# A three-block network in exact-split fp32: block boundaries ordered by token tile

## The reference, cut to what matters

```python
h = h + rms_norm(attention(rms_norm(h, g0)) @ w_o, g1)
h = h + rms_norm(square(relu(rms_norm(h, g2) @ w_up)) @ w_down, g3)
# layer 1: HGRN mixer, then gated MLP; layer 2: sparse attention (NSA), then gated MLP
x = x + gate * (hgrn(modulate(x, gain, shift, scale) @ w_in) @ w_out)
x = x + gate * ((silu(a) * b) @ ffn_out)      # a, b = split(modulate(x, ...) @ ffn_in)
kv = modulate(x, kv_norm, kv_shift, kv_scale) @ w_kv
x = x + gate * (nsa(modulate(x, ...) @ w_q, kv) @ w_out)
x = x + gate * ((silu(a) * b) @ ffn_out)
```

## Time and profile before

| | |
|---|---|
| median of 3 runs | 1187.85 us |
| the profiled execution, its own time | 1189.41 us |
| its span | 1187.6 us |
| TensorE busy | 1074.4 us, 90% of the span, 5987 matmuls |
| DVE busy | 782.2 us, 66% |
| ACT busy | 503.5 us, 42% |
| GpSimd busy | 87.4 us, 7% |
| mean granted TensorE clock | 0.955 of full speed |
| read from memory | 222.31 MB, 188 GB/s over the span |
| chain that ended last | TensorE 84%, DVE 9%, ACT 3% |

### The profile page before, as it was taken

The page is one execution under the profiler, slowest core; times in us unless marked ns, Lnnn a source line. Parts: engine busy times, 40 slices in busy tenths (PEclk is TensorE's granted clock), DMA queues, the critical chain, the costliest instruction groups (busy, mean ns, idle before and its releaser), DMA issues.

```text
span 1187.6 us, 15875 instructions
## 1 busy us (share of the span) xinstructions
PE 1074.4 (90%) x5987; PEld 893.3 (75%) x5987; DVE 782.2 (66%) x1033; ACT 503.5 (42%) x631; POOL 87.4 (7%) x108
## 2 busy tenths in 40 slices
PE   4998799999968997878899999779987997999997
PEld 3887578888857886767788888679864876888885
DVE  5777557766757589766678778788665556445553
ACT  6435254444443746422433333334155724444441
POOL 1000100000010003630000000000210200000000
PEclk9999989999998999989999999979878998999999
DMA  9963438876656782023597898557132021656531
GB/s 315 350 230 107 159 123 330 286 286 219 240 202 213 248 288 67 2 72 107 178 331 274 287 314 271 215 202 243 50 126 72 2 99 43 212 188 201 192 126 71
DMA packets 125606, 224.00 MB, mean 189 GB/s; under 512 B 4760, under 2 KB 58232, under 8 KB 125560
## 3 DMA queue, kind: packets, MB, share of 16 engines
q1 hardware_dynamic: 124904, 221.02, 53.3%
q0 software_dynamic: 656, 2.36, 0.7%
HBM read 222.31 MB, written 1.05 MB: 188 GB/s over the span
## 4 chain that ended last, share of the span: by engine, by line
PE 84%; DVE 9%; ACT 3%; issue 2%; POOL 1%; DMA 1%; SPq 0%; POOLq 0%; DVEq 0%; ACTq 0%
PE psum L1434 80%; PE psum L1878 1%; DVE arena L984 1%; PE psum L1451 1%; PE psum L1731 1%; DVE res L1023 1%; DVE gain_b L1168 1%; DVE arena L1168 1%; DVE xlo L991 1%; PE psum L1623 1%; ACT whi L616 1%; DVE wlo L929 1%; DVE arena L1022 1%; DVE arena L986 0%; DVE adaacc L947 0%
## 5 line engine op out<-in xcount | busy, mean ns | idle before, releaser
L929 DVE TENSOR_TENSOR wlo<-raw,whi 128x2048 fp32r<-128x2048 f32 (+2 forms) x172 | 341.6, 2000 | 206.9 <-ACT whi L616 206.6
L616 ACT CAST whi<-raw 128x2048 fp32r<-128x2048 f32 (+2 forms) x172 | 286.4, 1671 | 219.9 <-PE psum L1434 213.0
L1434 PE MATMUL psum<-whi,xhi 128*128 128x512 f32 (+1 forms) x896 | 356.2, 398 | 18.8 <-DVE xlo L991 11.7
L1434 PE MATMUL psum<-wlo,xhi 128*128 128x512 f32 (+1 forms) x896 | 351.1, 392 | 0.0
L1434 PE MATMUL psum<-whi,xlo 128*128 128x512 f32 (+1 forms) x896 | 350.8, 392 | 0.0
L1434 PEld LDWEIGHTS psum<-whi,xhi 128*128 128x128 f32 x896 | 172.3, 192 | 54.4 <-issue 22.1
L1434 PEld LDWEIGHTS psum<-whi,xlo 128*128 128x128 f32 x896 | 172.0, 192 | 34.5
L1434 PEld LDWEIGHTS psum<-wlo,xhi 128*128 128x128 f32 x896 | 172.4, 192 | 32.1
L947 DVE SCALAR_TENSOR_TENSOR adaacc<-adaw,cact,adaacc 128x512 f32<-128x512 f32 x196 | 147.3, 751 | 6.4
L1434 PE MATMUL psum<-whi,hhi 128*128 128x512 f32 x304 | 119.4, 393 | 5.6 <-DVE hlo L1229 2.8
L1434 PE MATMUL psum<-whi,hlo 128*128 128x512 f32 x304 | 118.4, 390 | 0.0
(11 more groups left out here) (236 smaller groups left out, 1018.8 us busy)
## 6 DMA issues: line engine op xcount, KB each, us to landing
adaw<-in_ada_w SPq DMA_DIRECT2D x48, 1024.0 KB, 5.4
raw<-in_ffn_w_in SPq DMA_DIRECT2D x88, 512.0 KB
raw<-in_ffn_w_out SPq DMA_DIRECT2D x44, 512.0 KB
raw<-in_w_up SPq DMA_DIRECT2D x16, 1024.0 KB
raw<-in_w_down SPq DMA_DIRECT2D x16, 1024.0 KB
raw<-in_hgrn_w_in SPq DMA_DIRECT2D x16, 1024.0 KB
raw<-in_attn_w_qkv SPq DMA_DIRECT2D x12, 1024.0 KB
adaw<-in_kv_ada_w SPq DMA_DIRECT2D x8, 1024.0 KB, 5.2
```

The source lines that it names most:

```text
L616: sc.copy(whi[:, s, 0:width], raw[:, s, 0:width]).then_inc(hi_ready[s], 1)
L929: ve.tensor_tensor(wlo[:, s, 0:width], raw[:, s, 0:width], whi[:, s, 0:width].bitcast(F32), ALU.subtract).then_inc(lo_ready[s], 1)
L1434: return te.matmul(dst, lhsT, rhs, start=start, stop=stop, skip_group_check=open_)
```

## The change

The work at the boundaries is ordered by token tile instead of by slot.

- `accumulate` and the last down step (`down_tiles`) do all of K for tile 0, then all of K for tile 1. The slots are used in both passes and are free (`used`) only in the second.
- The transposes of tile 0 (`norm(j, 0)`) stand ahead of the last slot of tile 1. `up_tiles` does the whole first `up` step for tile 0, then tile 1's transposes (and the gate's matmuls), then tile 1, into the banks 0 and 1, which tile 0's residual has left; `open_acc` moves behind this block. `project_tiles` does slots 0 and 1 of tile 0, tile 1's transposes, slots 2 and 3 of tile 0, then tile 1.
- A PSUM bank of transposes now holds four channel groups of one tile. `affine` works on 128x128 pieces, sixteen for a norm instead of eight; high and low parts are 4x128.
- DVE's order at A, C, E: residual of tile 0, split(0), scale and norm of tile 0, split(1), residual of tile 1, its norm, splits 2 and 3. At B and D split(2) and split(3) stand between the norms of tile 0 and tile 1. ACT's and GpSimd's orders follow.
- At A and B the multiply by the gain comes ahead of 1/rms, which goes into the addition (`scalar_tensor_tensor`); ACT's square goes to `junk`, not `y`.
- The last block of each MLP is written out behind the loop: its hidden transposes (and the ada sum at D) stand between the two slots of the down step before.

```diff
-            def accumulate(n, turned, m=None, gated=None):
-
-                for s in range(4):
-                    item_ready(s, n)
-                    pe.wait_ge(t_x, 4 * turned + s + 1)
-                    for i in range(TT):
+            def accumulate(n, turned, j, m=None, gated=None):
+
+                for i in range(TT):
+                    for s in range(4):
+                        if i == 0:
+                            item_ready(s, n)
+                            pe.wait_ge(t_x, 4 * turned + s + 1)
                         for f in range(2):
...
+                        if i == 1:
+                            ins.then_inc(used[s], 1)
+                        elif s == 3:
                             ins.then_inc(acc_done, 1)
...
+                        if i == 1 and s == 2:
...
+                            norm(j, 0)
...
+            def up_tiles(n, j, fresh, gated=None, gates=0):
+
+                for i in range(TT):
+                    if i == 1:
+                        norm(j, 1)
+                        if gated is not None:
+                            gate(gated, gates)
+                    for s in range(2):
+                        item_ready(s, n)
+                        pe.wait_ge(n_x, 4 * fresh + 2 * i + s + 1)
...
+            def project_tiles(n, j, fresh, width=512):
+
+                norm(j, 0)
+                for i in range(TT):
+                    for p in range(2):
+                        for half in range(2):
...
+                        if i == 0 and p == 0:
+                            norm(j, 1)
...
+            def down_tiles(n, kts, h0, low):
+
+                for i in range(TT):
+                    for s in (2, 3):
+                        item_ready(s, n)
+                        pe.wait_ge(h_lo, low[s - 2])
...
-            pe.wait_ge(h_lo, 2 * N_FF1)
-            down(Q_FF1 + N_FF1 - 1, 2, last=True)
-            norm(2, ada_upto=A_HIN)
+            up(Q_FF1 + N_FF1 - 1)
+            pe.wait_ge(h_lo, 2 * (N_FF1 - 1))
+            down(Q_FF1 + N_FF1 - 2, 2, slots=(2,))
+            ada(A_HIN - 1)
+            hidden1(N_FF1 - 1)
+            down(Q_FF1 + N_FF1 - 2, 2, slots=(3,))
+            down_tiles(Q_FF1 + N_FF1 - 1, 2, 0, (2 * N_FF1 - 1, 2 * N_FF1))
+            project_tiles(Q_HIN, 2, 2)
```

More of the change, by code:

```diff
@@ L713, in mlp1 @@
                     act.wait_ge(h_sq, 2 * t + b + 1)
+                    if last and b == 1:
+                        act.wait_ge(used[3], t + Q_FF1)
                     sc.copy(hhi[:, 2 * b:2 * b + 2, :], sq[:, 2 * b:2 * b + 2, :]).then_inc(h_hi, 1)
@@ L800, in _, with up_starts, mlp2 @@
             turn(1)
[L801 to L807, removed]
+            def up_starts(q0, k, j):
+                norm_square(j, 0)
+                split(0, q0)
+                split(1, q0)
+                norm_high(k, 0)
+                norm_square(j, 1)
+                norm_high(k, 1)
+                split(2, q0, 1024)
+                split(3, q0, 1024)
+            up_starts(Q_F2A, 3, 3)
+            def mlp2(t, q0, hb, first=False, nxt=2048, last=False, end=False):
                 if not last:
@@ L1082, in _ @@
             ada(A_WO, 1)
+            ada_save(A_WO)
+            chain(ve.tensor_copy(gs[:], vcol[:, 8:16]))
+            residual(0, 0)
             split(0, Q_FF1)
+            norm_scale(1, 0)
+            normed_tile(1, 1, 0, False)
             split(1, Q_FF1)
-            ada_save(A_WO)
-            residual(0)
-            chain(ve.tensor_copy(gs[:], vcol[:, 8:16]))
-            norm(1, 1, shift=False)
+            residual(0, 1)
+            norm_scale(1, 1)
+            normed_tile(1, 1, 1, False)
             split(2, Q_FF1)
@@ L1201, in _, with up_starts, mlp2 @@
             ada(A_HOUT, 1)
[L1202 to L1203 removed]
+            gate_save(0)
             ada_save(A_HOUT)
[L1205 to L1212 removed]
+            def up_starts(q0, k, j, g):
+                residual(j - 1, 0)
+                split(0, q0)
+                norm_scale(j, 0)
+                normed_tile(k, j, 0)
+                split(1, q0)
+                residual(j - 1, 1)
+                norm_scale(j, 1)
+                normed_tile(k, j, 1)
+                gate_save(g)
+                split(2, q0, 1024)
+                split(3, q0, 1024)
+            up_starts(Q_F2A, 3, 3, 1)
+            def mlp2(t, q0, hb, gb, m=None, first=False, nxt=2048, last=False, end=False):
                 if not last:
@@ L1259, in _ @@
                 ada_save(A_KV + t)
-            for b in range(4):
-                low(5, b)
+            for i in range(TT):
+                for g in range(2):
+                    low(5, i, g)
             for s in (2, 3):
@@ L1424, in _ @@
                 mlp2(t, Q_F2B, HT_F2B, 2 * N_FF2)
-            mlp2(N_FF2 - 1, Q_F2B, HT_F2B, 2 * N_FF2, last=True)
-            residual(5)
+            mlp2(N_FF2 - 1, Q_F2B, HT_F2B, 2 * N_FF2, last=True, end=True)
+            residual(5, 0)
+            residual(5, 1)
         @block.tensor
@@ L1598, in up, with down @@
                     ins.then_inc(used[s], 1)
-            def down(n, kts, last=False, slots=(2, 3)):
+            def down(n, kts, slots=(2, 3)):
                 for s in slots:
@@ L1721, in _ @@
             turn(1, hin[:, 0, :, :], r_n)
-            accumulate(Q_HOUT, 1, A_HOUT, 0)
-            gate(1, 1)
-            norm(3, gates=2)
+            accumulate(Q_HOUT, 1, 3, A_HOUT, 0)
             def mlp2_hidden(t, gb):
```

365 lines of the change are left out of this document (206 added, 159 removed).

## The result

The changed kernel takes **1194.75 us** (median of 4 runs, 1194.54 to 1195.0); the kernel before, run beside it, 1187.67 (1186.47 to 1188.0). The ratio is 1.0062, 95% interval 1.0044 to 1.0079: slower by 0.6%, where 0.4% faster was forecast, outside the range. The profiled execution has a span of 1192.7 us (its own time 1194.54), 5.1 more than before's 1187.6. Busy times moved little: TensorE 1084.1 us (9.7 more for the same 5987 matmuls, which take longer at the low clock), DVE 791.0 (8.8 more), ACT 503.2, GpSimd 84.0.

A forecast was written before the change was run, and what follows sets the result against it. TensorE, the busiest engine, was taken as held up by waits at block boundaries. Terms 0.9 + 2.0 + 4.2 - 0.3 - 2.6 + 1.3 - 0.5 gave 5.0 us off 1187.85: 1182.8, range 1176 to 1188.5.

The forecast's parts named there:

- A: Boundary from attention output to MLP 1: 4.2 us faster, with w_down landing at about 34.3 and low clock costing 2.6.
- C: Boundary from HGRN output to the first gated MLP: 0.9 us faster, next block starting 48.5 after its projection.
- E: Boundary from NSA output to the last MLP: 2.0 us faster, a gain of 2.3 less 0.3 of clock.
- B: Boundary from MLP 1 to HGRN input: 0.3 us slower, gain 2.3 against 2.6 of low clock after a 5 us wait.
- D: Boundary from gated MLP to KV: 2.6 us slower, ada sum 0.4 later after 6 us idling, low clock 2.2.
- F: End of the kernel, last down step and residual additions: 1.3 us faster.
- I charge 0.4: Clock cost in us at C for waits of 2.6 and 1.4 us, since the clock held through similar idling before.
- where before it waited 2.8 ahead of it: the step ends as before: Last down step at B: TensorE's wait for the split, 2.5 us, moves into tile 0's middle without delaying the step's end.
- All other loops keep their order and cost nothing: Loops away from the boundaries, untouched by the change: claimed to add 0 us.
- H: Untouched HGRN stretch, from the end of the second HGRN projection to the HGRN output's first matmul: change of 0.
- N: Untouched NSA stretch, from the end of the second KV projection to the NSA output's first matmul: change of 0.
- The slower rival: Whole kernel 1193.7 us by the clock alone, falling before tile 1's transposes, with more costly restarts; chance 0.09.

The follow-up runs named there:

- the late sum: Changed kernel with the ada sum moved on TensorE from between the first and second projections of B and D into the second: 1182.12 us, ratio 0.9944.
- the delay: Changed kernel with 8 matmuls of constants added behind the second HGRN projection, where TensorE never waits: 1194.65 us, ratio 1.0055.
- two other kernels: Changed kernel with ada sum moved, matmuls of constants and SP's order at A: 1164.5 us; the same with DVE's residual and split order also changed: 1171.17 us.

## Why the prediction was wrong

Three steps of the sum failed. The low clock behind short waits was priced at 0.4 and 0.3 us at C and E, and at nothing in B's last down step. The load of `w_down` at A was timed too early. The loops that the change does not touch were put at nothing and lost 2.9 us. The new waits for the ada sum, which make B and D losses, were forecast.

**F, the row scales and the arithmetic of durations** held: 1.3 us at F; sixteen scale-and-shifts 5.19 us (counted 5.4). Up to the next block, C (48.6 against 48.5) and E (2.3 us gained, as counted) held too. C's gain up to there is 0.9 and not 1.3, though: the block before the change began at 49.5, and the prediction took 49.8 from the chain.

**C and E: the step "I charge 0.4" (and 0.3) for the clock.** It was argued from the earlier trace rows, where the clock stayed at 1.00 for 6 us of a gap. It stayed there again through both half-tiles, but at C it fell in between, behind the first short wait (0.2 us), and at both it fell behind the second: the next blocks cost 1.6 and 2.1 us more. C came out at -0.7 for 0.9, E at 0.2 for 2.0. The bound "3.2 slower" held the case; the value taken was wrong. The experiment with matmuls of constants shows it: C takes 59.4 and E 56.8, against 60.5 and 60.3 before.

**A: the load term and the clock.** Restart of tile 1 at 39.4, not 37.7, because `w_down` landed 8.06 us after its issue at 144.05, at 36.1 and not at 34.3; 2.9 us of low clock, not 2.6. So A gave 2.2 of 4.2. That this load holds tile 1 back is shown by the run with SP's order changed, which gives 3.3 us at A.

**B: "where before it waited 2.8 ahead of it: the step ends as before".** The wait moved into the middle of the step, and its second part ran cold: 36 matmuls took 10.08 instead of 8.2.

```profile
338.01 0.50 PE L1486 MATMUL psum<-whi,hhi 128*128 128x512 f32 x1 [2.19 <-DVE wlo L950]
```

Tile 0 took 8.33, not 7.4. Of those 2.8 us 2.1 arrive at the end of the ada sum, through DVE's queue; the wait for the sum itself is what the prediction had named (4.9 us; 5 counted). -2.7 for -0.3, outside the bound given for B (1.2 slower).

**D** came as told: wait 5.9 (6), TensorE's restart 0.2 off once D's later start is set right, cold matmuls 2.8 for 2.2: -3.3 for -2.6.

Of the signs that were named, the split of slot 2 at A ended at 154.0 (153), and the waits for the transposes' rows stayed under 3.5 us but for D's (3.8). One sign of being wrong came: the clock fell inside a half, in tile 0's part of B's down step.

**"All other loops keep their order and cost nothing".** They keep their order, and H and N lost 1.3 and 1.6 us. Over thirteen profiles H took 118.5 to 122.4 us with one and the same code; N took 137.1 to 138.8 in the eight without the late sum. For H the rows of the granted clock (0.94, 0.92 and 0.94 with the delay; 1.00 against 0.58 in one stretch of two other kernels) show that this is the clock: the stretch waits for DVE again and again, and whether its matmuls run at 1.2 or 2.4 GHz depends on when they come. For N the rows agree (0.88 and 0.87, 1.6 us more of busy time for the same matmuls), but no run was made that tests it alone. No row of the trace before priced this.

The errors add up: start +1.3, A -2.0, B -2.4, H -1.3, C -1.6, D -0.7, N -1.6, E -1.8, F 0.0, together -10.1, from 5.0 faster to 5.1 slower. Of the 11.4 us on the wrong side 1.7 are the load at A and 0.4 the misread start of C's next block; nearly all of the rest is low clock, with N's share by the same reading as H's. The 1.3 at the start are luck on the other side. The slower rival (1193.7) was nearest in time and had 0.09, too little: its mechanism, more cold restarts than before, is right. That its number is so near is partly luck: it had C and E 2.5 and 2.4 us too slow, and the 2.9 us of H and N at nothing. The clock did fall before tile 1's transposes at C, as it said, but only 0.2 of its 1.25 us stood in the chain. The rule that was set against the forecast, bursts with waits between pay once per burst (the Trainium skill, TensorE: Matmul & The Clock Gate, HAM oscillation), agrees with B here (granted clock 0.83, 0.67 and 0.74 behind three waits) and with C (0.61 and 0.87 behind the two waits of 2.3 us), and only in part with A and E, where two or three waits cost one ramp, behind the longest at A and the last at E. The page tells it of waits longer than the 2.2 and 2.3 us here.

The larger omission is another: a named wait of 11 us was priced and left standing. The prediction took as given that `ada` stands between the projections; asked whether it must, a few more lines of the change would have been worth 12.6 us.

## What to carry to other kernels

When work is moved earlier on the bounding engine, follow the next operation in its queue that waits for a slower queue (here the ada sum): its time does not move, and what was gained becomes a wait, plus the cold matmuls behind it. Move that operation too. Splitting one long gap in short ones need not save the clock: waits of 2.2 and 2.3 us were followed by a ramp here too. Try matmuls of constants in the waits; they gave 1% even to the kernel before. Stretches with the same code moved by up to 4 us, 0.3% of this kernel: judge a small change by a table of stretches with their granted clock, not by the sum alone.

## What the runs showed of the hardware

- Matmuls whose result nobody reads hold the granted clock: 1.00 in place of 0.66 to 0.87 at five places of A, B and C, at 0.16 us for a bf16 matmul with 384 columns.
- A wait of 2.19 us in a stretch of otherwise full work (B's down step) was followed by a granted clock of 0.83 over the next 10 us; in one profile of the same code up to there (B and D by slot) the same wait had no cost, 8.50 us for the 36 matmuls.
- The same code took 118.5 us at a mean granted clock of 0.96 or 122.4 at 0.92 (H), and an added delay of 1.3 us was free.
- GpSimd's first operation of an rsqrt, on 128x1, took 1.39 us under DVE's weight split (141.20 to 143.48, both inputs in SBUF), where it took 0.19 under the multiply that reads PSUM:

```profile
142.15 1.39 POOL L518 TENSOR_SCALAR stat<-stat 128x1 f32<-128x1 f32 x1 [9.09 <-ACT arena L638]
```
